# Half-block products in the first feed-forward, and another order of VectorE's attention work

## The reference, cut to what matters

```
def swiglu(x, wi, wo):
    a, b = jnp.split(x @ wi, 2, axis=-1)
    return (jax.nn.silu(a) * b) @ wo
h = h + 0.5 * rmsnorm(swiglu(rmsnorm(h, n[0]), ffn1_wi, ffn1_wo), n[1])
```

```
p = jax.nn.softmax(jnp.where(mask, logits, -jnp.inf), axis=-1)
outs.append(jnp.einsum('bhts,bhsd->bhtd', p, vh[:, :, :end]))
```

## Time and profile before

| what | value |
| --- | --- |
| median of 3 runs | 3122.79 us (3119.26 to 3123.34) |
| the profiled execution's own time | 3116.99 us |
| its span in the trace | 3115.2 us |
| PE busy | 3044.7 us, 98% |
| DVE busy | 1932.5 us, 62% |
| ACT busy | 1236.5 us, 40% |
| POOL busy | 664.8 us, 21% |
| mean TensorE clock granted | 0.998 of full speed |

### The profile page before, as it was taken

One profiled execution on the slowest core, in us unless ns is written; L12 is line 12 of the kernel. 1 busy time (PEld: TensorE's weight loads), 2 busy tenths in 40 slices (PEclk: granted clock), 3 DMA queues, 4 the chain that ended last, 5 costly groups with the idle time before them and its releaser, 6 DMA issues. The chain is left out here.

```text
span 3115.2 us, 54978 instructions
## 1 busy us (share of the span) xinstructions
PE 3044.7 (98%) x21809; PEld 2805.7 (90%) x21809; DVE 1932.5 (62%) x3550; ACT 1236.5 (40%) x1948; POOL 664.8 (21%) x549
## 2 busy tenths in 40 slices
PE   8998999999999999999999999999999999999999
PEld 8976789999999999999999999998888788778887
DVE  7344489988888868888885333354356376563343
ACT  4235423457777633333334312332233344343232
POOL 0010205763333333433320101101000021301011
PEclk9999999999999999999999999999999999999999
DMA  4210224679999999999982322222222100223232
GB/s 157 82 41 1 83 81 147 200 289 340 333 339 343 349 336 352 350 356 362 354 297 83 106 78 91 95 79 86 98 75 81 29 4 10 88 82 114 82 100 70
DMA packets 160169, 517.34 MB, mean 166 GB/s; under 512 B 18929, under 2 KB 51825, under 8 KB 156657
## 3 DMA queue, kind: packets, MB, share of 16 engines
q1 hardware_dynamic: 75632, 279.93, 26.3%
q0 software_dynamic: 44032, 159.40, 14.7%
q10 hardware_dynamic: 40320, 75.52, 6.6%
HBM read 462.35 MB, written 52.43 MB: 165 GB/s over the span
## 5 line engine op out<-in xcount | busy, mean ns | idle before, releaser
L185 DVE TENSOR_TENSOR w_lo<-ring,w_hi 128x1024 fp32r<-128x1024 f32 (+2 forms) x157 | 205.9, 1312 | 546.7 <-ACT w_hi L179 546.7
L179 ACT ACTIVATE w_hi<-ring 128x1024 fp32r<-128x1024 f32 (+2 forms) x170 | 190.1, 1118 | 433.5 <-PE ps L245 359.8
L245 PE MATMUL ps<-f_hn_hi,w_hi 128*128 128x264 f32 (+1 forms) x1056 | 280.5, 319 | 0.8 <-DVE w_lo L185 0.6
L245 PE MATMUL ps<-f_hn_hi,w_lo 128*128 128x264 f32 (+1 forms) x1056 | 279.8, 319 | 0.0
L245 PE MATMUL ps<-f_hn_lo,w_hi 128*128 128x264 f32 (+1 forms) x1056 | 279.8, 319 | 0.0
L486 ACT ACTIVATE w_hi<-ring 128x1024 fp32r<-128x1024 f32 x170 | 180.1, 1059 | 224.4 <-PE ps L543 220.8
L490 DVE TENSOR_TENSOR w_lo<-ring,w_hi 128x1024 fp32r<-128x1024 f32 x144 | 176.4, 1225 | 111.3 <-ACT w_hi L486 111.1
L514 PE MATMUL ps<-hn_hi,w_hi 128*128 128x384 f32 x680 | 231.8, 341 | 2.4 <-POOL w_lo L490 2.4
L543 PE MATMUL ps<-units_hi,w_hi 128*128 128x384 f32 x680 | 227.6, 335 | 2.2 <-DVE units_lo L868 2.2
L514 PE MATMUL ps<-hn_lo,w_hi 128*128 128x384 f32 x680 | 227.6, 335 | 0.0
L514 PE MATMUL ps<-hn_hi,w_lo 128*128 128x384 f32 x680 | 227.6, 335 | 0.0
(11 more groups left out here) (520 smaller groups left out, 8000.4 us busy)
## 6 DMA issues: line engine op xcount, KB each, us to landing
ring<-in_w_uv SPq DMA_DIRECT2D x256, 512.0 KB, 6.1
ring<-in_f_up SPq DMA_DIRECT2D x88, 512.0 KB, 3.5
expert_units<-scratch ACTq DMA_DIRECT2D x128, 192.0 KB, 5.0
gate_table<-peer ACTq DMA_DIRECT2D x24, 1024.0 KB, 8.2
peer<-gate_table POOLq DMA_DIRECT2D x64, 384.0 KB, 8.8
peer<-expert_units ACTq DMA_DIRECT2D x128, 192.0 KB, 5.9
ring<-in_w_in SPq DMA_DIRECT2D x29, 512.0 KB, 3.5
ring<-in_w_late SPq DMA_DIRECT2D x25, 512.0 KB, 3.5
```

The source lines that it names most:

```text
L179: self.nc.scalar.activation(self.h[:, self.slot(k), 0:self.cols], e.ring[:, self.ring(k), 0:self.cols], ACT.Copy).then_inc(e.hi_done, 1)
L185: self.nc.vector.tensor_tensor(self.l[:, self.slot(k), 0:self.cols], e.ring[:, self.ring(k), 0:self.cols], self.h[:, self.slot(k), 0:self. ...
L245: mm = nc.tensor.matmul(e.ps[:, bank + hf, 0:tokens.width], lhsT[:, wt.slot(k), col], rhs(part, c)[:, cut], start=(c == 0 and j == 0), sto ...
```

## The change

**Up products.** A new class `Seven` takes the first feed-forward in place of `Ffn`. A pair's weights are seen as a 2x2 of quarters (a1, a2: the gate tile's halves of the contraction; b1, b2: the linear tile's) and the input as a 2x2 too (halves of the contraction by halves of the tokens, x11, x12, x21, x22). Their product is made of seven products of quarters in place of eight. Four of the weights used are sums: s1 = b1+b2, s2 = s1-a1, s3 = a1-b1, s4 = a2-s2, made for every block by POOL (`mixes`, 128x512 each) into the unused end of each ring slot; the input's sums t1 to t4 (128x1056 each) are made once, t1 and t2 by DVE, t3 and t4 by POOL. Each of the 7 products ("units") of a block has its own weights of 128x512, its own `hi` (ACT, `whi`) and `lo` (DVE, `wlo`), 7 deep, and 12 matmuls of 264 tokens in a bank of its own. The results are put together by ACT (`hold`) and DVE (`c11`, `u2`, `u3`, `p5`, `fin`) before factor, silu and product. The second multiplication by the factor (`gate`) goes to POOL, except for the last block of a round. The sums of squares of the norm go from DVE to POOL.

**Rounds.** The 22 blocks are cut 8, 8, 6 in place of 12, 10 (three times 8 down tiles); the ring's tiles and the host's layout follow. All loops of this stage are written out. ACT and DVE follow the units in one list; while PE is at unit n they split unit n+7.

**Attention.** DVE's order at step n becomes recip(n), scale(n), max(n+1).

Of the new class the core is shown; left out are `orders`, which only numbers the steps for the semaphores, the names of tiles and slots, the start of each engine's program (gains, t1 to t4, the 7 operands of 128x1056 with `op_hi` on ACT and `op_lo` on DVE, each ahead of its unit's `whi` and `wlo`), and the reads of PSUM after a down tile.

```diff
+class Seven:
...
+    RING = 7
...
+    def sp(self, sp):
+        e = self.e
+        for t, (name, k, _) in enumerate(self.tiles):
+            if t >= SLOTS:
+                sp.wait_ge(self.ready, self.tiles[t - SLOTS][2])
+                cols = e.w[name].shape[2]
+                sp.dma_start(e.ring[:, self.slot(t), 0:cols], e.w[name][k]).then_inc(e.slot_full[self.slot(t)], 16)
+        nxt, n = self.nxt[self.names[-1]], len(self.tiles)
+        for k in range(SLOTS):
+            sp.wait_ge(self.ready, self.tiles[n - SLOTS + k][2])
+            sp.dma_start(e.ring[:, self.slot(n + k), 0:e.w[nxt].shape[2]],
+                         e.w[nxt][k]).then_inc(e.slot_full[self.slot(n + k)], 16)
+        sp.sem_inc(e.lo_done, n)
+    def pe_pair(self, pe, q):
+        r, j, n, _ = self.pairs[q]
+        for i in range(self.RING):
+            pe.wait_ge(self.ready, n + i + 1)
+            if q == 0:
+                self.after_dve(pe, "op", i)
+            if j == 0 and r > 0:
+                self.after_dve(pe, "sum", r - 1, 4 + i // 2)
+            elif j > 0 and i == 0:
+                self.after_act(pe, "x", q - 1)
+            elif j > 0:
+                self.after_dve(pe, ("c11", "u2", "p5", "u3", "fin", "fin")[i - 1], q - 1)
+            if q == 1 and i == 6:
+                self.front.pe_rooted(pe)
+            at = (n + i) % self.RING
+            for c in range(DC // 2):
+                for m, (part, w) in enumerate(((0, 0), (1, 0), (0, 1))):
+                    mm = self.nc.tensor.matmul(self.e.ps[:, i, 0:HL], self.w[w][:, at, c * P:(c + 1) * P],
+                                               self.op[part][:, i, c], start=c == 0 and m == 0,
+                                               stop=c == DC // 2 - 1 and m == 2)
+            mm.then_inc(self.used, 1)
+            if q == 1 and i == 3:
+                self.after_dve(pe, "fin", 0)
+                self.front.pe_total(pe)
+    def pe_down(self, pe, r, k):
+        blocks, n = SEVENS[r], self.tiles[self.pairs[self.first[r] + SEVENS[r] - 1][3] + 2 + k][2] - 2
+        bank, last = 2 * (k % SLOTS), self.first[r] + blocks
+        if k < 3:
+            self.after_dve(pe, ("c11", "p5", "fin")[k], last - 1)
+        elif k == 3 and r == 0:
+            self.after_dve(pe, "fin", last - 1)
+        elif k == 3:
+            self.after_dve(pe, "sum", r - 1, 7)
+            self.after_dve(pe, "fin", last - 1)
+        else:
+            self.after_dve(pe, "sum", r, k - 4)
...
+    def whi(self, act, n):
+        kind, i, h = self.units[n]
+        if n >= self.RING:
+            act.wait_ge(self.used, n - self.RING + 1)
+        if kind == "up" and h in (2, 3, 4, 5):
+            self.after_pool(act, "mix", i, {3: 0, 2: 1, 4: 2, 5: 3}[h])
+        else:
+            self.wait_tile(act, self.tile_of(n))
+        src, cols = self.source(n)
+        self.nc.scalar.activation(self.w[0][:, n % self.RING, 0:cols], src, ACT.Copy).then_inc(self.unit_hi, 1)
+    def wlo(self, dve, n):
+        dve.wait_ge(self.unit_hi, n + 1)
+        src, cols = self.source(n)
+        self.nc.vector.tensor_tensor(self.w[1][:, n % self.RING, 0:cols], src,
+                                     self.w[0][:, n % self.RING, 0:cols].bitcast(F32),
+                                     ALU.subtract).then_inc(self.ready, 1)
...
+        def hold(q):
+            act.wait_ge(self.used, self.pairs[q][2] + 1)
+            if q > 0:
+                self.after_dve(act, "u2", q - 1)
+            A_(self.kept, e.ps[:, 0, 0:HL], ACT.Copy).then_inc(self.by_act, 1)
...
+        for c in range(4, DC):
+            A_(self.y[:, c], e.h[:, c], ACT.Copy, scale=self.gain[:, c:c + 1]).then_inc(self.by_act, 1)
+        for i in range(3):
+            op_hi(i)
+            self.whi(act, i)
+        hold(0)
+        for i in range(3, 7):
+            op_hi(i)
+            self.whi(act, i)
+        self.whi(act, 7)
+        squares(0)
+        self.whi(act, 8)
+        squares(1)
+        for n in range(9, self.RING + 7):
+            self.whi(act, n)
+        for n, (kind, i, h) in enumerate(self.units):
+            if kind == "up" and i > 0 and h == 0:
+                hold(i)
+            if n >= 7 and n + self.RING < len(self.units):
+                self.whi(act, n + self.RING)
+            if kind == "up":
+                if i == 1 and h == 3:
+                    self.front.act_root(act)
+                elif i == 1 and h == 5:
+                    silu(0)
+                elif i == 2 and h == 0:
+                    g_hi(0)
+                elif i > 1 and h == 1 and not self.ends(i - 1):
+                    g_hi(i - 1)
+                elif i > 0 and h == 6:
+                    silu(i)
+                    if self.ends(i):
+                        g_hi(i)
+            elif i >= DC * (len(SEVENS) - 1) and h == 1:
+                k = i % DC
+                if k == 0:
+                    self.close.act_table(act)
+                self.after_dve(act, "sum", i // DC, k)
+                self.close.act_square(act, k)
...
+        def c11(q):
+            dve.wait_ge(self.used, self.pairs[q][2] + 2)
+            self.after_act(dve, "x", q)
+            if q > 1:
+                self.after_dve(dve, "both", q - 1)
+            V.tensor_tensor(self.quarters(q)[:, 0], e.ps[:, 1, 0:HL], self.kept, ALU.add).then_inc(self.by_dve, 1)
+        def u2(q):
+            dve.wait_ge(self.used, self.pairs[q][2] + 3)
+            V.tensor_tensor(self.quarters(q)[:, 1], e.ps[:, 2, 0:HL], self.kept, ALU.add).then_inc(self.by_dve, 1)
+        def u3(q):
+            s = self.quarters(q)
+            dve.wait_ge(self.used, self.pairs[q][2] + 5)
+            self.after_dve(dve, "u2", q)
+            V.tensor_tensor(s[:, 2], e.ps[:, 4, 0:HL], s[:, 1], ALU.add).then_inc(self.by_dve, 1)
+        def p5(q):
+            s = self.quarters(q)
+            self.after_dve(dve, "u3", q)
+            V.tensor_tensor(s[:, 1:4:2], e.ps[:, 3:4, 0:HL].broadcast_to([P, 2, HL]), s[:, 1:3],
+                            ALU.add).then_inc(self.by_dve, 1)
+        def fin(q):
+            s = self.quarters(q)
+            dve.wait_ge(self.used, self.pairs[q][2] + 7)
+            self.after_dve(dve, "p5", q)
+            V.tensor_tensor(s[:, 1:3], e.ps[:, 5:7, 0:HL], s[:, 1:3], ALU.add).then_inc(self.by_dve, 1)
+        def scale(q):
+            self.after_dve(dve, "fin", q)
+            x = self.first_half(q)
+            V.tensor_tensor(x, x, e.r1, ALU.mult).then_inc(self.by_dve, 1)
+        def both(q):
+            self.after_act(dve, "silu", q)
+            if q > 1:
+                self.after_pool(dve, "low", q - 2)
+            y = self.prod[:, q % 2]
+            V.tensor_tensor(y, self.second_half(q), self.first_half(q), ALU.mult).then_inc(self.by_dve, 1)
+            if self.ends(q):
+                self.after_dve(dve, "both", q)
+                V.tensor_tensor(y, y, e.r1, ALU.mult).then_inc(self.by_dve, 1)
...
+        for i in range(4):
+            op_lo(i)
+            self.wlo(dve, i)
+        c11(0)
+        op_lo(4)
+        self.wlo(dve, 4)
+        u2(0)
+        op_lo(5)
+        self.wlo(dve, 5)
+        op_lo(6)
+        self.wlo(dve, 6)
+        u3(0)
+        p5(0)
+        fin(0)
+        for n in range(7, 14):
+            self.wlo(dve, n)
+        for n, (kind, i, h) in enumerate(self.units):
+            if kind == "up" and i > 0:
+                if h == 1:
+                    c11(i)
+                elif h == 2:
+                    u2(i)
+                elif h == 4:
+                    u3(i)
+                    p5(i)
+                elif h == 6:
+                    fin(i)
+                    scale(i)
+                    if self.ends(i):
+                        both(i)
+            if kind == "down" and h == 1:
+                k = i % DC
+                dve.wait_ge(self.used, n + 1)
+                z, y = EVERY.banks(e, 2 * (k % SLOTS)), halves(self.y[:, k])
+                if i < DC:
+                    V.tensor_copy(y, z).then_inc(self.by_dve, 1)
+                else:
+                    V.tensor_tensor(y, y, z, ALU.add).then_inc(self.by_dve, 1)
+            if n >= 7 and n + self.RING < len(self.units):
+                self.wlo(dve, n + self.RING)
+            if kind == "up":
+                if i == 1 and h == 4:
+                    self.front.dve_scale(dve)
+                    scale(0)
+                elif i == 1 and h == 5:
+                    both(0)
+                elif i > 0 and h == 6 and not self.ends(i):
+                    both(i)
...
+        def mixes(q):
+            r, j, n, t = self.pairs[q]
+            self.wait_tile(pool, t)
+            self.wait_tile(pool, t + 1)
+            a, b = (e.ring[:, self.slot(t + i)] for i in range(2))
+            s1, s2, s3, s4 = self.parts
+            old = self.pairs[q - 1][2] if q else None
+            if q:
+                pool.wait_ge(self.ready, old + 4)
```

(64 more changed lines are left out.)

164 lines of the change are left out of this document (added).

## The result

The changed kernel takes 3176.1 us (median of 4 runs, 3171.8 to 3179.9) where the kernel before takes 3123.1 beside it: a ratio of 1.0167 [1.0151, 1.0184]. Slower was forecast, but 3137 in a range of 3112 to 3156; the loss is 53 us, not 14. The profiled execution takes 3177.85 us with a span of 3176.0, so 60.8 more than the span before.

A forecast was written before the change was run, and what follows sets the result against it. PE was taken to bound the feed-forward, hand-overs attention. Terms -31.7 + 42 + 7.5 + 2.8 + 3.8 - 1.5 made +23, attention -8.5: +14.5 on 3117.0, plus 5.8 to the median, 3137 us; range 3112 to 3156.

The forecast's parts named there:

- Attention -8.5: Attention: scale ahead of max shortens the chain between items; 8.5 us less, bounds 4 to 11 less.
- The chain over two items: Attention, single heads: mix, turn, scores, max to soft, soft, evac and hand-over take 5.3 us, 2.65 an item, not 3.12.
- Fewer matmuls -31.7: First feed-forward: 84 matmuls a block in place of 96, 264 fewer at 0.12 us, 31.7 us less.
- Start +42: Round 0 of the up products: late first product and DVE and POOL taking turns delay the blocks; 42 us more.
- Rounds 1 and 2, +7.5 and +2.8: Later up products: sums 12.4 us apart against PE's 10.08 a block; 7.5 and 2.8 us more.
- Ends of rounds +3.8: First down tile of each round: last block's 5.8 us chain outlasts PE's other work by 0.8, 0.8, 2.2: 3.8 us more.
- The start's port: Stage start: the four gain multiplications on DVE may contend with POOL, making the start some 4 us later.
- The signs named: Feed-forward: `wlo` near 1.0, POOL's sums above 1.5, PE idle about 70 us, 50 in round 0, POOL busy above 160.
- C: Attention gains nothing, since `soft` waits for `scale` and `max` what `turn` saves: +8.5, 3145 us; chance 0.10.
- A: Up products: POOL frees the port early, PE stays the bound, 10.1 us a block: 3113 us; chance 0.13.
- B: Stage start: the port holds, but the start is 12 to 15 us shorter: about 3123 us; chance 0.17.
- D: Up products: DVE and POOL wait out full durations, 13.6 us a block, start 6 later: 3156 us; chance 0.10.

The follow-up runs named there:

- Late look-ahead: Changed kernel, but in a round's last block DVE makes five down-tile low weights only after that block's product and factor: 3164.0 us, ratio 1.0146.
- 40: Changed kernel with 40 unneeded 128-column matmuls ahead of PE's wait for the last low part in each round's first down tile: 3176.5 us.
- 24 matmuls alone: Changed kernel with 24 unneeded 128-column matmuls ahead of PE's wait for the last low part in each round's first down tile: 3165.6 us.
- the factor on DVE alone: Changed kernel with the second factor multiplication of every block on DVE, not on POOL: 3170.7 us, ratio 1.0152.
- with the doubled addition: Changed kernel with every block's second factor on DVE and the third unit's 264-column PSUM addition done twice in all blocks but the first: 3172.5 us.

## Why the prediction failed

Against the terms of its sum, in the profiled execution:

- **Attention -8.5**: -9.1. The chain over two items, 5.3 us, is 5.31. Alone it brings 7.3 in the medians.
- **Fewer matmuls -31.7**: as said; PE's 10.1 to 10.2 us a block is confirmed without sums (81.7 for 8).
- **Start +42**: round 0 lasts 131.2 for PE's own 83.8, +47.4. The first product at 14.6 us lay at the end of 11 to 15. 25 of it go with POOL's sums, shown by leaving them out; how much of that is hold-up and how much the order of steps was not taken apart. The sum had no term for the clock: 7.6 us by the four stretches at 0.50, more than the 5.4 by which the term was short.
- **Rounds 1 and 2, +7.5 and +2.8**: +10.8 and +5.1. The period was 12.77, not 12.4, within the bounds 11.6 to 13.6. The price was near, in part by luck, and the reason half right: the turns make DVE's operations longer, as the Trainium skill says (SBUF — State Buffer, "Who interferes with whom"), and this trace shows it with 1.77 for 0.69. But what sets the period is DVE's order, 8.1 of its own and 4.3 held, not the sum over the port, in which the additions from PSUM would be free.
- **Ends of rounds +3.8**: 55.6 - 46.1, 55.7 - 46.1, 44.0 - 34.6 = **+28.5. This is the step that failed**, 25 of the 35 us by which the stage was missed. The chain behind the last addition was priced right at 5.8 (1933.55 to 1939.26 is 5.7). Two things were left out. First, the chain was set from PE's last up matmul, but DVE reaches the last addition only 5.8 us after it: in a period that DVE fills, it ends the round behind, with the look-ahead for the down tiles still in line. The rows (last up matmul, four low parts of the look-ahead, last addition):

```profile
1927.71 0.28 PE L1423 MATMUL ps<-f_op_hi,f_w_lo 128*128 128x264 f32 x1
...
1930.06 1.28 DVE L1473 TENSOR_TENSOR f_w_lo<-ring,f_w_hi 128x512 fp32r<-128x512 f32 x2
...
1932.35 1.28 DVE L1473 TENSOR_TENSOR f_w_lo<-ring,f_w_hi 128x512 fp32r<-128x512 f32 x2
1933.55 0.70 DVE L1600 TENSOR_TENSOR scratch<-ps,scratch 128x528 f32<-128x528 f32 x1
```

  The 0.8, 0.8 and 2.2 were waits of 5.7, 5.8 and 6.5. Late look-ahead gets back 1.7 to 2.7 of each. Second, behind such a wait PE works at granted clock 0.50 for the next 5 to 6 us; keeping PE at work brings 2.2 to 2.6 a round. About 1 us a round is not accounted for.
- **The start's port**: the gains were to cost some 4 us beside POOL's sums. The prediction named them and left them out of its sum. The runs agree: the four take 4.76 us with the sums and 1.71 without, POOL's first sum takes 1.56, and the first product comes 4.0 us sooner without the sums.

```profile
1649.88 4.76 DVE L1618 TENSOR_SCALAR f_y<-h,param_tab 128x528 f32<-128x528 f32 x4 [0.30 <-PEq L1739]
```

- **Clock elsewhere**: the sum supposed the clock of the execution before. The stretch at 0.50 ahead of attention stood in 6 of 14 profiles: those of the changed kernel, of the one without sums, of 40 and of 24 matmuls alone, of the factor on DVE alone and with the doubled addition; not in the other eight, among them the products alone and attention alone. What the change does cannot be its cause by itself, since kernels with both parts lie on either side. Why one program or execution falls into it is open, and with it some 8 us of the 60.8. So are the 5 us behind the feed-forward.
- **The signs named**: low weights near 1.0 (1.08), POOL's sums above 1.5 (1.65) and POOL above 160 us busy (220) came true. PE's idle time did not: 60 us in the stage where 70 were named, 32 before the end of round 0 where 50 were. The stage is longer than forecast with less idle time, since part of the loss is work at half the clock.

Of the rivals none held. C (attention gains nothing) is refuted by the -9.1; A (port not full) and B (short start) stood on the wrong side; D (13.6 a block) came nearest in time by a mechanism that the period rules out.

## What to carry over

Before work is moved from PE to engines that feed it, add up each engine's line in order, with the time that it is held by a neighbour, not only its own durations: here POOL was idle a quarter of the steady period and DVE, whose operations it held, was full. Where one phase runs with a helper engine at its limit, that engine is late when the phase ends, and the hand-over starts from its clock, not PE's; every such join here also paid for the low clock behind its wait. The 31.7 us of matmuls saved stand against a start of 47 us, 16 of lag in the two later rounds and three joins of 9.5.
